# Weight slabs split two at a time, and an exclusive decay made by a quotient, in a hybrid encoder layer

## The reference

```
h = x + 0.5 * rms(swiglu(rms(x), ffn1_w_in, ffn1_w_out))
z = rms(h) @ w_in                       # 5376 columns: attention q, k, v | rwkv | gates
A = differential attention(z)           # 4 heads, two softmax maps, chunks of 64
B = RWKV-7 time mixing(z)               # 8 heads of 64
h = h + rms((sig(gA) * (A @ w_o_att) + sig(gB) * (B @ w_o_rwkv)) @ w_out)
y = h + 0.5 * rms(swiglu(rms(h), ffn2_w_in, ffn2_w_out))
```

## Time and profile before

| | |
|---|---|
| median of 3 runs | 3088.08 us |
| profiled execution | 3096.12 us |
| its span, first to last instruction | 3094.3 us |
| TensorE matmul / weight load busy | 3007.3 us (97%) / 2668.6 us (86%) |
| VectorE / ScalarE / GpSimd busy | 1727.8 us (56%) / 1350.4 us (44%) / 398.6 us (13%) |
| instructions TensorE / VectorE / ScalarE | 23912 / 3052 / 2730 |
| mean granted TensorE clock | 0.987 of full |

### The profile page before, as it was taken

One profiled execution on the slowest core, in us unless ns is written; L12 is line 12 of the kernel. 1 busy time (PEld: TensorE's weight loads), 2 busy tenths in 40 slices (PEclk: granted clock), 3 DMA queues, 4 the chain that ended last, 5 costly groups with the idle time before them and its releaser, 6 DMA issues.

```text
span 3094.3 us, 59121 instructions
## 1 busy us (share of the span) xinstructions
PE 3007.3 (97%) x23912; PEld 2668.6 (86%) x23912; DVE 1727.8 (56%) x3052; ACT 1350.4 (44%) x2730; POOL 398.6 (13%) x738
## 2 busy tenths in 40 slices
PE   8999999999999999999999999999999999999997
PEld 8999988888878778998888788888888989899997
DVE  5445543644574464474675655646856846656444
ACT  4335444532444433443444444444545434554333
POOL 1001001211321210210211101201112100010000
PEclk9999999998999999999999999999999999999999
DMA  5445556643664564652654643625655424665443
GB/s 167 128 128 169 162 171 219 216 153 108 214 194 145 177 197 147 213 157 88 213 184 158 203 142 120 190 80 177 197 160 159 146 90 142 203 208 170 126 127 122
DMA packets 504495, 500.54 MB, mean 162 GB/s; under 512 B 29096, under 2 KB 402112, under 8 KB 504208
## 3 DMA queue, kind: packets, MB, share of 16 engines
q1 hardware_dynamic: 475968, 406.36, 41.6%
q0 software_dynamic: 28256, 90.39, 9.5%
HBM read 443.16 MB, written 54.47 MB: 161 GB/s over the span
## 4 chain that ended last, share of the span: by engine, by line
PE 91%; DVE 4%; ACT 1%; issue 1%; DMA 1%; POOL 1%; SPq 0%; ACTq 0%; DVEq 0%; POOLq 0%
PE ps L280 44%; PE ps L290 30%; PE ps L1094 5%; PE ps L1861 1%; PE ps L1880 1%; PE ps L1795 1%; PE ps L302 1%; PE ps L1099 1%; PE ps L1086 1%; PE ps L1806 1%; DVE wlo L244 1%; PE ps L1832 1%; PE ps L1226 1%; PE ps L1872 1%; PE ps L1818 1%
## 5 line engine op out<-in xcount | busy, mean ns | idle before, releaser
L244 DVE TENSOR_TENSOR wlo<-raw,whi 128x512 fp32r<-128x512 f32 x1140 | 783.9, 690 | 853.5 <-ACT whi L236 850.8
L236 ACT ACTIVATE whi<-raw 128x512 fp32r<-128x512 f32 x1140 | 713.0, 628 | 600.5 <-PE ps L280 356.1
L280 PE MATMUL ps<-xnhi,whi 128*128 128x384 f32 x2688 | 930.7, 346 | 5.0 <-DVE xnlo L557 5.0
L280 PE MATMUL ps<-xnhi,wlo 128*128 128x384 f32 x2688 | 904.1, 336 | 0.0
L280 PE MATMUL ps<-xnlo,whi 128*128 128x384 f32 x2688 | 903.9, 336 | 0.0
L280 PEld LDWEIGHTS ps<-xnhi,whi 128*128 128x128 f32 x2688 | 508.8, 189 | 31.3 <-issue 18.2
L280 PEld LDWEIGHTS ps<-xnlo,whi 128*128 128x128 f32 x2688 | 508.8, 189 | 3.2 <-issue 2.6
L280 PEld LDWEIGHTS ps<-xnhi,wlo 128*128 128x128 f32 x2688 | 508.2, 189 | 0.0
L290 PE MATMUL ps<-whi,hidhi 128*128 128x512 f32 x936 | 384.3, 411 | 16.8 <-DVE xnlo L557 11.1
L290 PE MATMUL ps<-whi,hidlo 128*128 128x512 f32 x936 | 368.9, 394 | 0.0
L290 PE MATMUL ps<-wlo,hidhi 128*128 128x512 f32 x936 | 368.3, 393 | 0.0
(11 more groups left out here) (323 smaller groups left out, 3269.4 us busy)
## 6 DMA issues: line engine op xcount, KB each, us to landing
raw<-in_ffn_w_in_dram SPq DMA_DIRECT2D x528, 256.0 KB, 2.9
raw<-in_ffn_w_out_dram SPq DMA_DIRECT2D x264, 256.0 KB, 2.6
raw<-in_w_in_dram SPq DMA_DIRECT2D x252, 256.0 KB, 2.9
xt<-h_scratch SPq DMA_DIRECT2D x42, 512.0 KB, 5.9
att<-in_cache_att_k_dram POOLq DMA_DIRECT2D x64, 256.0 KB, 5.0
att<-in_cache_att_v_dram POOLq DMA_DIRECT2D x64, 256.0 KB, 3.2
rw<-zr_scratch POOLq DMA_DIRECT2D x51, 256.0 KB, 7.2
raw<-in_w_out_dram SPq DMA_DIRECT2D x48, 256.0 KB, 2.6
```

The lines of the kernel that those rows point to most:

```text
L236: act.activation(B["whi"][:, slot], B["raw"][:, slot], ACT.Copy).then_inc(E["whi"], 1)
L244: dve.tensor_tensor(B["wlo"][:, slot], B["raw"][:, slot], B["whi"][:, slot].bitcast(F32), ALU.subtract).then_inc(E["wlo"], 1)
L280: ins = pe.matmul(ps[:, bank, 0:BT], B["w" + wt][:, n % RING, i * P:(i + 1) * P], x(xt, i), start=first and i == 0 and (wt, xt) == passes[ ...
```

## The change

Three things are changed together.

1. ScalarE and VectorE handle two slabs per instruction (1024 elements per partition). One semaphore count now stands for a pair. ScalarE waits for both loads of a pair, which share a semaphore. The steps stand at even slabs, three ahead of the first slab of the pair, and two pairs are made before the first stage instead of three slabs.
2. The rings: high and low parts have six buffers (three pairs) instead of five, raw slabs four (two pairs) instead of five. SP runs 6 slabs ahead instead of 7.
3. The exclusive product: the strictly triangular matmul and its matrix are gone. ScalarE makes `exp(0.5 * KAPPA * (S_TW + 1))`, the inverse of the token's own decay, and VectorE multiplies it by the inclusive product `S_E1` before `S_AT` is made.

```diff
-RING = 5
+RING = 6
+RAW = 4
 ...
 def weights_sp(sp, B, E, t):
     for n, src in enumerate(weight_slabs(t)):
-        slot = n % RING
-        if n >= RING:
-            sp.wait_ge(E["wlo"], n - RING + 1)
+        slot = n % RAW
+        if n >= RAW:
+            sp.wait_ge(E["wlo"], (n - RAW) // 2 + 1)
 ...
-        sp.dma_start(dst, src).then_inc(E["raw_in%d" % slot], 16)
+        sp.dma_start(dst, src).then_inc(E["raw_in%d" % (slot // 2)], 16)
 ...
 def weights_act(act, B, E):
-    for n in range(FIRST[-1]):
-        slot = n % RING
-        act.wait_ge(E["raw_in%d" % slot], 16 * (n // RING + 1))
+    for n in range(0, FIRST[-1], 2):
+        slot, raw = n % RING, n % RAW
+        act.wait_ge(E["raw_in%d" % (raw // 2)], 32 * (n // RAW + 1))
         if n >= RING:
-            act.wait_ge(E["used"], n - RING + 1)
-        act.activation(B["whi"][:, slot], B["raw"][:, slot], ACT.Copy).then_inc(E["whi"], 1)
+            act.wait_ge(E["used"], n - RING + 2)
+        act.activation(B["whi"][:, slot:slot + 2], B["raw"][:, raw:raw + 2], ACT.Copy).then_inc(E["whi"], 1)
 ...
 def weights_dve(dve, B, E):
-    for n in range(FIRST[-1]):
-        slot = n % RING
-        dve.wait_ge(E["whi"], n + 1)
-        dve.tensor_tensor(B["wlo"][:, slot], B["raw"][:, slot], B["whi"][:, slot].bitcast(F32), ALU.subtract).then_inc(E["wlo"], 1)
+    for n in range(0, FIRST[-1], 2):
+        slot, raw = n % RING, n % RAW
+        dve.wait_ge(E["whi"], n // 2 + 1)
+        dve.tensor_tensor(B["wlo"][:, slot:slot + 2], B["raw"][:, raw:raw + 2], B["whi"][:, slot:slot + 2].bitcast(F32), ALU.subtract).then_inc(E["wlo"], 1)
 ...
 # u_slab and x_slab
-        pe.wait_ge(E["wlo"], n + 1)
+        pe.wait_ge(E["wlo"], n // 2 + 1)
 ...
 # rw_pe
         yield "G"
-        pe.wait_ge(*done(E, "gg", p + 1))
-        pe.matmul(ps[:, RB[0], :], B["tri"][:, 2 * kd + 1], slot(S_TW), start=True, stop=True).then_inc(E["rw_mm"], 1)
         yield "CX"
 ...
 # rw_act
-        act.wait_ge(*done(E, "cx", p + 1))
+        act.wait_ge(*done(E, "th", 2 * p + 1))
         act.wait_ge(E["rw_mix"], 3 * p + 3)
-        act.activation(slot(S_EP), b0, ACT.Exp, scale=-0.5 * KAPPA, bias=rc[:, 12 + 3 * kd:13 + 3 * kd]).then_inc(E["rw_kept_a"], 1)
+        act.activation(slot(S_EP), slot(S_TW), ACT.Exp, scale=0.5 * KAPPA, bias=rc[:, 14:15]).then_inc(E["rw_kept_a"], 1)
 ...
 # rw_dve
         dve.wait_ge(*done(E, "ep", p + 1))
+        own.do(dve.tensor_tensor(slot(S_EP), slot(S_EP), slot(S_E1), ALU.mult))
         dve.scalar_tensor_tensor(slot(S_AT), slot(S_KN), -1.0, slot(S_EP), ALU.mult, ALU.mult).then_inc(E["rw_kept_v"], 1)
 ...
 # weave, for ScalarE and VectorE
-        for n in range(issued, FIRST[-1]):
+        for n in range(issued, FIRST[-1], 1 if queue else 2):
             events[max(-1, n - ahead)].append("weights")
 ...
 # scalar and vector: two pairs up front instead of three slabs
-                for _ in range(AHEAD):
+                for _ in range(AHEAD // 2 + 1):
                     next(weights)
 ...
 # sync
-                for _ in range(RING):
+                for _ in range(RAW):
                     next(weights)
-                weave({...}, 2, AHEAD + RING - 1, True, RING)
+                weave({...}, 2, AHEAD + RAW - 1, True, RAW)
```

More of the change, by code:

```diff
@@ L138, in buffers @@
         B["w" + h] = sb("w" + h, [P, RING, 512], F32R)
-    B["raw"] = sb("raw", [P, RING, 512])
+    B["raw"] = sb("raw", [P, RAW, 512])
     B["yb"] = sb("yb", [P, NT, D])
@@ L154, in buffers @@
     B["lw"] = sb("lw", [P, 3, 512])
-    B["tri"] = sb("tri", [P, 4, P])
+    B["tri"] = sb("tri", [P, 2, P])
     B["mk"] = sb("mk", [P, 2, 5, 64])
     B["rc"] = sb("rc", [P, 84])
-    B["rs"] = sb("rs", [P, 96])
+    B["rs"] = sb("rs", [P, 80])
     B["att"] = sb("att", [P, 8704])
@@ L1019 @@
 RW_ORDER = {
-    "rw_mm": ("lf wa wa g ci cx pd fa fb fk fr mab qa qk s2 x2 mvp s4 x3 s8 x4 hh htp r2 xtp r3 wp v0 v1",
+    "rw_mm": ("lf wa wa g ci pd fa fb fk fr mab qa qk s2 x2 mvp s4 x3 s8 x4 hh htp r2 xtp r3 wp v0 v1",
         "us ss us ss yy",
@@ L1121, in rw_pe @@
         pe.wait_ge(*done(E, "th", 2 * p + 2))
-        pe.matmul(ps[:, RB[1], :], B["tri"][:, 2 * kd], slot(S_TW), start=True, stop=True).then_inc(E["rw_mm"], 1)
+        pe.matmul(ps[:, RB[1], :], B["tri"][:, kd], slot(S_TW), start=True, stop=True).then_inc(E["rw_mm"], 1)
         yield "G"
-        pe.wait_ge(*done(E, "gg", p + 1))
-        pe.matmul(ps[:, RB[0], :], B["tri"][:, 2 * kd + 1], slot(S_TW), start=True, stop=True).then_inc(E["rw_mm"], 1)
         yield "CX"
@@ L1335, in rw_act @@
         act.wait_ge(E["rw_mix"], 3 * p + 2)
[L1336 to L1337 removed]
+        act.activation(slot(S_E0), b1, ACT.Exp, scale=0.5 * KAPPA, bias=rc[:, 10 + 2 * kd:11 + 2 * kd]).then_inc(E["rw_kept_a"], 1)
+        act.activation(slot(S_E1), b1, ACT.Exp, scale=-0.5 * KAPPA, bias=rc[:, 11 + 2 * kd:12 + 2 * kd]).then_inc(E["rw_kept_a"], 1)
         yield "G"
[L1339 removed]
+        act.wait_ge(*done(E, "th", 2 * p + 1))
         act.wait_ge(E["rw_mix"], 3 * p + 3)
[L1341 removed]
+        act.activation(slot(S_EP), slot(S_TW), ACT.Exp, scale=0.5 * KAPPA, bias=rc[:, 14:15]).then_inc(E["rw_kept_a"], 1)
         yield "CX"
@@ L2264, in init_pool @@
     pool.dma_start(B["rc"][:, :], t["c_rc"]).then_inc(E["late_in"], 16)
-    pool.dma_start(B["tri"][:, :, :], t["c_tri"].rearrange("p (i c) -> p i c", i=4)).then_inc(E["late_in"], 16)
+    pool.dma_start(B["tri"][:, :, :], t["c_tri"].rearrange("p (i c) -> p i c", i=2)).then_inc(E["late_in"], 16)
     pool.dma_start(B["mk"][:, :, :, :], t["c_masks"].rearrange("p (a b c) -> p a b c", a=2, b=5)).then_inc(E["late_in"], 16)
@@ L2468, in _ @@
                 next(dense)
-                weave({"weights": weights, "dense": dense, "norm": norm, "rw": rw_act(act, B, E), "att": att_act(act, B, E), "late": late_act(act, B, E)}, 1, AHEAD, False, AHEAD)
+                weave({"weights": weights, "dense": dense, "norm": norm, "rw": rw_act(act, B, E), "att": att_act(act, B, E), "late": late_act(act, B, E)}, 1, AHEAD, False, AHEAD + 1)
             @block.vector
@@ L2482, in _ @@
                 next(dense)
-                weave({"weights": weights, "dense": dense, "norm": norm, "rw": rw_dve(dve, B, E), "att": att_dve(dve, B, E), "late": late_dve(dve, B, E)}, 1, AHEAD, False, AHEAD)
+                weave({"weights": weights, "dense": dense, "norm": norm, "rw": rw_dve(dve, B, E), "att": att_dve(dve, B, E), "late": late_dve(dve, B, E)}, 1, AHEAD, False, AHEAD + 1)
             @block.gpsimd
@@ L2505, in _ @@
                 weights = weights_sp(sp, B, E, t)
-                for _ in range(RING):
+                for _ in range(RAW):
                     next(weights)
-                weave({"weights": weights, "norm": norm, "dense": dense, "gates": gates_sp(sp, B, E, t)}, 2, AHEAD + RING - 1, True, RING)
+                weave({"weights": weights, "norm": norm, "dense": dense, "gates": gates_sp(sp, B, E, t)}, 2, AHEAD + RAW - 1, True, RAW)
                 for tl in range(NT):
@@ L2547, in constants @@
         inside_of = i[:, None] // size == i[None, :] // size
-        tri += [inside_of & (i[:, None] <= i[None, :]), inside_of & (i[:, None] < i[None, :])]
-        bias += [0.5 * KAPPA * (i % size + 1), -0.5 * KAPPA * (i % size + 1), -0.5 * KAPPA * (i % size)]
+        tri.append(inside_of & (i[:, None] <= i[None, :]))
+        bias += [0.5 * KAPPA * (i % size + 1), -0.5 * KAPPA * (i % size + 1)]
+    bias.append(0.5 * KAPPA)
     rc = np.zeros((P, 84), f)
```

## The result

| | before | after |
|---|---|---|
| median | 3089.76 us (3087.87 to 3091.66, 4 runs) | 3117.85 us (3110.92 to 3124.28, 4 runs) |
| ratio after / before | | 1.0085, 95% interval 1.0070 to 1.0099 |
| profiled execution, span | 3096.12 us, 3094.3 us | 3110.92 us, 3109.1 us |

The forecast was 3082 us with a range from 3071 to 3098. The profiled execution of after is the shortest of its four, so the trace shows 14.8 us of growth of the span, not all of the 28. All lines of after stand one higher than before up to L1123 (L236 is L237, L244 is L245, L290 is L291).

The account below looks back on a forecast made before the run. The prediction took TensorE, busy 97% of the span, as the bound. Its terms, -7.7 (matmul gone), +0.5 (start), +2.3 (raw buffers), -1.0 (pairs), sum to -5.9 off 3088.08: 3082 us, range 3071 to 3098.

Parts of the forecast that it names:

- What bounds it: Whole kernel: TensorE, busy 97% of the span; an edit pays only if TensorE gets less to do or waits less.
- Part 1: RWKV tiles: dropping the exclusive-sum matmul saves 0.86 us in each of 9, -7.7 us; VectorE's added multiply counted 0.
- Rival (b): RWKV tiles: the removed matmul's time turns into waiting, so -7.7 becomes about 0, 3090 us; chance 0.20.
- Part 2: ScalarE's and VectorE's weight splitting: high and low parts in pairs give -1 us, bounds -9 to +6.
- every second step has none, nor its wait: ScalarE's and VectorE's queues: a pair holds an engine 1.0 to 1.2 us, but every other step has no weight instruction.
- Part 3: Weight rings: raw buffers 5 to 4, high and low 5 to 6; +2.3 us near slab 552, bounds 0 to +5.
- 2.0 us or a little more to spare: Raw loads with four buffers: margin left before a pair needs its second load, where it was 6 us.
- a landing of twice the median: Raw loads: landing that slowly makes ScalarE wait, with `xnhi`, gates' tanh, RWKV and attention copies queued behind it.
- The path: First OP entry: slab 552's pair, late behind `xt` loads, is ready at 1524.0 against TensorE's need at 1521.76, +2.3 us.
- TensorE's waits as a whole move by over 6 us: Sign, over the whole run: such a move either way would show the forecast wrong.
- Rival (c): Three OP entries: four raw buffers too few, TensorE waits and its clock drops, 7.5 us each, +14, 3102 us; chance 0.15.
- Start, +0.5: Kernel start: four slabs instead of three split before the first `xnlo` delay TensorE's first matmul by 0.5 us (0 to 1.5).

Follow-up runs that it names:

- e1: The kernel before with the quotient (item 3 of the change) alone, slabs one at a time, five raw and five split buffers: 3085.85 us, ratio 0.9985.
- e3: The kernel after with six raw buffers instead of four, both engines in pairs, attention weights moved to make room: 3093.11 us, ratio 1.0003.
- e4: e1 with six raw buffers instead of five, slabs one at a time, five split buffers: 3086.73 us, ratio 0.9982.
- e9: e3 with VectorE making one slab at a time, ScalarE still in pairs, six raw and six split buffers: 3083.35 us, ratio 0.9963.
- e14: e4 with six split buffers instead of five, both engines one slab at a time: 3083.71 us, ratio 0.9981.
- e2: e1 with four raw buffers instead of five, slabs one at a time: 3093.08 us, ratio 1.0007.
- e11: After with six raw buffers, without GpSimd's loads at the head of RWKV tiles 1 to 8 (zeros written instead): 3068.78 us, ratio 0.9926.

## Why the prediction was wrong

- **What bounds it.** Right that only TensorE's work and waits count: 197 us of the weights' bars taken off VectorE and ScalarE bought nothing.
- **Part 1, -7.7.** Alone the quotient measured -4.6 (1.9 to 7.4), and one more matmul a tile +5.6. The starts of the earlier trace rows give the time in that place; some of it comes back as waits later (TensorE's waits are 74.3 us in e1, 70.4 before). Rival (b) is partly true. Mis-sized by 2 to 3 us, harmless.
- **Part 2, -1.0, bounds -9 to +6.** Wrong sign: e3 against e4 is +6 us. The step that failed is "every second step has none, nor its wait": on VectorE the relief in one step doesn't pay for 0.6 us more in the other (e9 against e3, 10 to 12 us). That VectorE's results for TensorE come in every step is my reason for it, not a run's. The fixed price per instruction of the Trainium skill (VectorE: DVE Perf Modes, "The TRN2 errata — SBUF-src ops pay a fixed extra latency per instruction") shows in bars: 111 us less on ScalarE, where the estimate by it was 106, but 86 us on VectorE, where it was 34 (1140 x 690 ns against 570 x 1224). On VectorE it was rightly given no share of the time; on ScalarE e9 and e14 leave it open between nothing and some 6 us.
- **Part 3, the step that decided.** Four raw buffers were priced at +2.3 us and cost 25 (after against e3). "2.0 us or a little more to spare" was right as a median, and was then priced at one place of the three entries. It rested on the landing of 2.9 us in the earlier trace rows, a median over 528 loads, while before's own trace has 6.0 us beside tile 0's loads: there 2.0 to spare is 1.1 short. The prediction's own condition, "a landing of twice the median", was met there. It took the crowding only where `xt` is loaded and not where GpSimd loads, nine times. SP's queue may add to it: its waits for gates that ScalarE makes went from 22.8 to 62.7 us in its list of waits, with ScalarE in pairs (65.8 in e3, 52.7 in e9) and not in singles (23.1 in e2). A gate behind a pair would be late, and the next raw load stands behind its store; what that costs was not measured apart.
- **The path.** I priced a late pair by when TensorE needs the weights: "+2.3 us" against a need at 1521.76. No such wait came: neither the matmuls nor the weight loads wait for `wlo` there. The sentence that named what stands behind in ScalarE's queue was there, and no term of the sum came from it. At this entry the stage before it lost 8.4 us, through the 4.19 us for `LT` and the half clock behind it. The sign "TensorE's waits as a whole move by over 6 us" came, with 24.8 us.
- **Rival (c), 0.15.** Right in its cause, four raw buffers too few, and its sign. Wrong in place: the second and the third OP entry (each OP stage with the one ahead of it) came to -0.7 and +2.4 us, while the first IP stage, where tile 0 is loaded, lost 5.3. Wrong in its evidence against, TensorE's 0.8 us for `wlo`, which measures the other side of the ring. Its price of 7.5 us for one entry, wait and clock together, is near the 8.4 us of the first. What it said of the clock agrees at one place: after the 4.19 us stop TensorE runs at 0.51 for 6.1 us. The Trainium skill's rule that waits between bursts put TensorE back to half its clock (TensorE: Matmul & The Clock Gate, "HAM oscillation — how this bites in real kernels") is borne out there, but as sum over the run the clock moved by 0.001.
- **Start, +0.5.** First L281 at 15.2 us, +0.4: right.

The sum by measured parts: -4.6 (quotient, e1), -1 (six raw buffers in singles, e4), +6.5 (pairs, e3), +25 (four raw buffers, after) is +26, as by the ratio. It closes by its making, since these are steps from one kernel to the next; in another order the parts are others (in singles four raw buffers cost 7 us). Why the plain runs of after are up to 13 us longer than its profiled one stays open.

## What to carry to other kernels

Size a load ring by the slowest landing it meets and not by the median: look up the landing in every stretch where another queue loads in bulk. A wait in an in-order queue is priced by what stands behind it, so ask which engine waits for the copy after the late one, before asking who waits for the late data. Instructions merged on an engine that serves the busy one every step can cost time even where they save its bars, as VectorE's did here; test such a change on each engine alone. Here the better kernel is the change with VectorE in singles and six raw buffers: 0.9963 (0.9949 to 0.9976) of before. Singles on both engines with the same buffers come close (0.9981).

## What the runs showed of the hardware

- SP's 256 KB raw loads land in 2.6 to 3.3 us (medians over the run, before and after), in 6.0 to 6.4 beside GpSimd's group of 8 loads of 256 KB and 3 of 128 KB, and in 9.5 with 1.5 MB of `xt` and 1.6 MB of attention loads in flight as well.
- After a stop of 4.19 us TensorE's granted clock was 0.51 from 1525.80 to 1531.90 us.
- Two slabs in one instruction: 1224 ns instead of 2 x 690 on VectorE, 1057 instead of 2 x 628 on ScalarE; three queued 128x512 subtractions take 1.90 us, 0.63 each.
- Half of the bytes in each raw load took off 63% of ScalarE's waits for them (122.6 to 45.8 us), not all.
- Taking away the loads of eight tiles (8 of 256 KB and 3 of 128 KB each) was worth 24 us even where ScalarE waits for raw only 6.5 us in all (e11 against e3): VectorE's waits for these inputs fell from 22.4 to 4.9 us, and a wait of TensorE of 5.0 us at L1795, for which the profile names no engine, is gone.
